# A two-layer MoE diffusion trunk: the last expert step of the second layer added by one-hot matmuls

## The chip, the cores and the metric

The kernel runs on one core of a Trainium2 chip. The metric is the device time of one execution in microseconds, as the median of several runs.

## What is computed

Two transformer layers over 128 context tokens and 512 latent tokens, 640 tokens of width 1024 in five tiles of 128 rows. All is float32. A layer is attention of three kinds and then a mixture of 16 experts, of which each token takes two. What matters here is the end of a layer and the final norm:

```python
x = x + gate2 * hier_moe(h, ...)          # each token: the sum of its two experts' rows
...
y_prompt = rms_norm(x_prompt, final_norm_g)
y_sample = rms_norm(x_sample, final_norm_g)
```

## The kernel before

PE is TensorE, DVE VectorE, ACT ScalarE, POOL GpSimd, SP the queue that issues most loads. The program is written out by hand for each engine, with semaphores between them; the order on an engine is the order of its code.

**Expert steps.** The 1280 pairs of token and expert are sorted by expert into slots, and 128 slots make a step. There are at least MIN_ET = 10 and at most N_ET = 18 steps; with this routing 15 are used in layer 0 and 14 (0 to 13) in layer 1. A step from 10 on stands under `if_used` (L493), a branch on the number of used steps; a skipped step still raises its semaphores by one (`else_inc`, L495 to L502). Step i does this:
- POOL gathers the 128 token rows from h_rows (L891).
- PE transposes them (`rows_T`), multiplies by the gate and up weights (`gate_up`, L2227, L2228 and L2233; a step of one expert has 8 matmuls of 128x512, one of two experts 16 on half the columns each), transposes the hidden rows (`hidden_T`), and multiplies by the down weights into PSUM banks 5 and 6 (`down`, L2268, L2269, L2275).
- DVE computes the hidden rows (`hidden`, L1743 to L1752), copies transposes (L1736, L1759), finishes the gate rows (L1763), and in `y_copy` (L1772) multiplies PSUM by slot weight and gate row into y_out[i % 2], two products of 128x512. Then y_evac_d counts i + 1.
- POOL's `y_store(i)` (L877) adds these rows to x_rows, the residual in HBM, by an indirect DMA with addition. It waits for y_evac_d and for the scatter before it, since two of them may hold the same token.

The loops are staggered: on DVE iteration i is `hiddenT(i-1)`, `rows_in(i+1)`, `hidden(i)`, `y_copy(i-1)`; on PE `gate_up(i)`, registers of step i + 1, `hidden_T(i-1)`, `rows_T(i+1)`, `down(i-1)`. `down(i)` waits for y_evac_d to reach i, since y_copy(i-1) reads the same banks. SP loads the experts' weights into four slots as the steps release them (L593, L597), and tells of their landing in order (L618).

**The end.** POOL waits for the landings of all used scatters and raises x_final (L907, L909). SP then loads the five tiles x_t from x_rows (L630), each with its own semaphore s_xin[t]. Per tile ACT sums squares (`final_sums`, L976), POOL forms the reciprocal root (L736, L741), DVE scales (`final_scale`, L1191), and SP stores the tile (L688).

The functions that the change touches follow, with the line numbers of the profile.

Of the kernel before, what the change touches and what calls it, by code (L numbers as in the profile page):

```python
# [21 lines left out]
P = 128  # L22
# [135 lines left out]
def trunk(nc, a, o):  # L158
# [9 lines left out]
    with ctx:  # L168
# [46 lines left out]
        rout_w = sb("rout_w", 2 * NT)  # L215
        tok_id = sb("tok_id", NT)
        lane = sb("lane", P)
        lane_w = sb("lane_w", 64)
        slots_i = sb("slots_i", 2 * NT, I32)
        w_slot = sb("w_slot", N_ET)  # L220
# [17 lines left out]
        b2b = arena[:, 2048:4096].rearrange("p (k n) -> p k n", k=2)  # L238
        gate2c = qT[:, 0:D]
        gain_f = arena[:, 0:1024]  # L240
        gain_b = q_tok[4]
        last_scaled = q_tok[4]
        a2b = arena[:, Q0 + 2 * D:Q0 + 4 * D].rearrange("p (k n) -> p k n", k=2)
# [51 lines left out]
        two = lane[:, 0:N_HALF:2]  # L295
        k_view = [k_tok[:, 640 * s:640 * (s + 1)] for s in range(2)]
        gate2l = modrow[:, 0:D]

        def hT_bank(t, r):
            return 1 if t == 0 and r == 1 else 7  # L300
# [392 lines left out]
        def _(pool):  # L693
            dma = pool.dma_start
            for v in (ident[:], wuk[:], sel64[:], k_tok[:]):
# [9 lines left out]
                      allow_small_or_imprecise_dtypes=True)  # L705
            pool.iota(k64, pattern=[[HALF, C_MAX]], base=0, channel_multiplier=0,
                      allow_small_or_imprecise_dtypes=True)
            pool.iota(tok_id[:], pattern=[[P, NT]], base=0, channel_multiplier=1,
                      allow_small_or_imprecise_dtypes=True)
            pool.iota(lane[:], pattern=[[1, P]], base=0, channel_multiplier=0,  # L710
# [71 lines left out]
            for l in range(DEPTH):  # L782
# [84 lines left out]

                def y_store(i):

                    with if_used(pool, i):  # L870
                        pool.wait_ge(y_evac_d[l], i + 1)
                        if i == 0:
                            pool.wait_ge(s_xout, (l + 1) * 16 * NT)
                        else:

                            pool.wait_ge(s_yout[l][(i - 1) % 2], 16 * ((i - 1) // 2 + 1))
                        pool.indirect_dma_start(  # L877
                            out=x_rows[l], out_offset=bass.IndirectOffsetOnAxis(ap=idx[:, i:i + 1], axis=0),
                            in_=y_out[i % 2], in_offset=None, compute_op=ALU.add
                        ).then_inc(s_yout[l][i % 2], 16)  # L880
# [22 lines left out]
                for i in range(N_ET - 3, N_ET):  # L903
                    y_store(i)

                for i in range(MIN_ET - 2, N_ET):
                    with if_used(pool, i):  # L907
                        pool.wait_ge(s_yout[l][i % 2], 16 * (i // 2 + 1))
                pool.sem_inc(x_final, 1)  # L909
                if l + 1 < DEPTH:  # L910
# [12 lines left out]
        def _(act):  # L923
# [48 lines left out]
                mod_copy(0, j)  # L972

            def final_sums(t):
                act.wait_ge(s_xin[t], 16 * DEPTH)
                act.activation(work[:, 1024 * (t % 2):1024 * (t % 2 + 1)], x_t[t], ACT.Square, scale=D ** -0.5,  # L976
                               accum_out=ssf[:, t:t + 1]).then_inc(f_ss, 1)
                act.drain()
# [196 lines left out]
        def _(dve):  # L1175
# [17 lines left out]
            for l in range(DEPTH):  # L1193
# [560 lines left out]
                def hiddenT(i):  # L1754
                    with if_used(dve, i):
                        dve.wait_ge(ht_done[l], i + 1)
                        if i >= 2:
                            dve.wait_ge(dn_done[l], i - 1)
                        cp(hidT[i % 2], ps[:, 4, 0:FF].rearrange("p (c n) -> p c n", c=2)).then_inc(ht_evac[l], 1)  # L1759

                        dve.wait_ge(lat_part[l], i + 1)
                        g = gate_rows[i % 2]
                        stt(g, gate2c, of_ctx[:, i:i + 1], g, ALU.mult, ALU.add)  # L1763

                def y_copy(i):
                    with if_used(dve, i):
# [2 lines left out]
                        y_buffer_free(dve, l, i)  # L1769
                        for k in range(2):  # L1770
                            half = slice(512 * k, 512 * (k + 1))
                            last = stt(y_out[i % 2][:, half], ps[:, 5 + k, :], w_slot[:, i:i + 1],  # L1772
                                       gate_rows[i % 2][:, half], ALU.mult, ALU.mult)
                        last.then_inc(y_evac_d[l], 1)
                    else_inc(dve, i, y_evac_d[l], 1, i)

# [2 lines left out]
                for i in range(N_ET + 1):  # L1779
# [8 lines left out]
                    if i >= 1:  # L1788
                        y_copy(i - 1)

            for t in range(NT):
                final_scale(t)


        @block.tensor
        def _(pe):
# [73 lines left out]
            for l in range(DEPTH):  # L1870
# [418 lines left out]
                for i in range(N_ET + 1):  # L2289
# [10 lines left out]
                    if i >= 1:  # L2300
                        down(i - 1)

_INS = ['x_prompt', 'x_sample', 'c', 'cache_mla_ckv', 'cache_mla_krope', 'cache_gqa_k', 'cache_gqa_v',
# [57 lines left out]
```

## Time and profile before

| | |
|---|---|
| median of 3 runs | 1450.79 us (1449.01 to 1451.2) |
| the profiled execution, its own time | 1446.95 us |
| its span | 1445.1 us |
| PE busy | 1269.4 us, 88% of the span |
| DVE busy | 728.3 us, 50% |
| ACT busy | 410.9 us, 28% |
| POOL busy | 226.9 us, 16% |

The profile is that of one execution; its times are counted from the start of its span. The shares are averages over stages with different limits: attention, weight loading and the expert steps each have their own. In the expert steps of layer 1, the last 190 us, the scatters follow each other at 11 to 19 us; the last two are at 1408 and 1416 us. A matmul of f32 operands stands in the profile as two records.

### The profile page before, as it was taken

What the parts mean: (1) busy time and instruction counts of PE and PEld (TensorE: products, weight loads), DVE (VectorE), ACT (ScalarE), POOL (GpSimd) and SP (SyncE); (2) the same over time, 40 slices, a digit from 0 to 9 for tenths busy, and PEclk for the clock granted to TensorE, in tenths of its full rate; (3) what the DMA queues carried; (4) which work ended last, traced back from release to release, by engine and by line L of the source; (5) the groups of instructions that cost most, each with busy time, mean ns of one, the idle gap of its engine ahead of it and who ended that gap; (6) DMA issues with size and microseconds to landing.
All of it is one profiled execution on the core that took longest, in us unless ns stands there. A gap on an engine that the chain in (4) does not pass through costs nothing. (4 is left out here: it accounts for less than half of the span.)

```text
span 1445.1 us, 22628 instructions
## 1 busy us (share of the span) xinstructions
PE 1269.4 (88%) x8172; PEld 758.8 (53%) x8172; DVE 728.3 (50%) x1741; ACT 410.9 (28%) x923; POOL 226.9 (16%) x325
## 2 busy tenths in 40 slices
PE   5899979999999959988959999899999992999981
PEld 4445546777767734433434554577776672444330
DVE  0344435776744545553514544466785437355442
ACT  2111135666610111111121110567664000111101
POOL 3310012010021112211111010210101111122212
PEclk8999999999999979999969999999999996999995
DMA  9800239000041797999950004670103233899955
GB/s 332 293 14 1 98 138 329 21 31 15 2 146 64 277 388 228 359 364 339 327 155 14 1 1 174 226 186 2 31 16 112 93 125 112 299 379 376 338 195 177
DMA packets 77996, 244.87 MB, mean 169 GB/s; under 512 B 9280, under 2 KB 19024, under 8 KB 65520
## 3 DMA queue, kind: packets, MB, share of 16 engines
q1 hardware_dynamic: 56080, 183.26, 34.1%
q0 software_dynamic: 17616, 58.44, 14.1%
q8 instruction: 101, 1.65, 0.5%
q10 hardware_dynamic: 4160, 1.20, 0.4%
q14 instruction: 39, 0.32, 0.1%
HBM read 213.54 MB, written 31.00 MB: 169 GB/s over the span
## 5 line engine op out<-in xcount | busy, mean ns | idle before, releaser
L1903 PE MATMUL ps<-ring,hT_region 128*128 128x512 f32 (+1 forms) x640 | 272.2, 582 | 3.4 <-ACT hT_region L988 3.4
L1903 PEld LDWEIGHTS ps<-ring,hT_region 128*128 128x128 f32 x640 | 121.6, 193 | 136.1 <-issue 135.5
L1352 DVE TENSOR_SCALAR_CACHE_REDUCE ring<-ps 128x768 f32<-128x768 f32 (+1 forms) x168 | 132.7, 820 | 119.1 <-PE ps L1976 92.6
L1041 ACT ACTIVATE ring<-ring,negm 128x768 f32<-128x768 f32 (+1 forms) x168 | 137.7, 820 | 30.9 <-DVE ring L1352 30.9
L2100 PE MATMUL ps<-ring,hT_region 128*128 128x384 f32 (+1 forms) x480 | 141.9, 452 | 0.0
L2233 PE MATMUL ps<-ring,hT_region 128*128 x272 | 125.4, 616 | 8.9 <-DVE hT_region L1736 4.6
L1976 PE MATMUL ps<-arena,qT 64*128 64x384 f32 (+1 forms) x640 | 124.8, 507 | 8.5 <-DVE ring L1352 2.9
L2100 PEld LDWEIGHTS ps<-ring,hT_region 128*128 128x128 f32 x480 | 89.6, 190 | 42.0 <-issue 0.3
L2029 PE MATMUL ps<-work,arena 128*64 128x128 f32 x1600 | 105.5, 278 | 6.0 <-ACT work L1057 4.3
L1057 ACT ACTIVATE work<-ps 128x512 f32<-128x512 f32 x128 | 75.8, 592 | 97.7 <-PE ps L1800 97.7
L2227 PE MATMUL ps<-ring,hT_region 128*64 x192 | 90.4, 626 | 13.4 <-SPq L618 13.4
L2029 PEld LDWEIGHTS ps<-work,arena 128*64 128x64 f32 x1600 | 86.1, 137 | 25.3 <-issue 15.0
L2233 PEld LDWEIGHTS ps<-ring,hT_region 128*128 128x128 f32 x272 | 52.8, 197 | 78.1 <-issue 78.1
L877 POOL DMA_INDIRECT x_rows<-arena,idx x29 | 47.0, 1620 | 297.1 <-DVE arena L1772 198.8
L1759 DVE COPY work<-ps 128x256 f32<-128x256 f32 x29 | 12.3, 424 | 161.2 <-PE ps L1800 161.2
L1137 ACT ACTIVATE work<-ps 128x256 f32<-128x256 f32 x29 | 11.1, 384 | 284.3 <-PE ps L2233 155.4
L2228 PE MATMUL ps<-ring,hT_region 128*64 128x512 f32 x192 | 90.4, 626 | 0.0
L1800 PE MATMUL ps<-ident,ring 128*128 128x128 f32 x600 | 82.3, 279 | 0.6 <-ACT work L1053 0.2
L1800 PEld LDWEIGHTS ps<-ident,ring 128*128 128x128 f32 x600 | 65.4, 141 | 28.6 <-issue 26.3
L1976 PEld LDWEIGHTS ps<-arena,qT 64*128 64x128 f32 (+1 forms) x640 | 56.1, 185 | 41.6 <-issue 18.5
L1227 DVE TENSOR_TENSOR work<-ps,rope 128x256 f32<-128x256 f32 (+2 forms) x40 | 14.0, 349 | 112.6 <-PE ps L1903 111.7
L2275 PE MATMUL ps<-arena,work 128*128 x136 | 64.5, 618 | 2.9 <-DVE work L1759 2.7
(322 smaller groups left out, 1776.8 us busy)
## 6 DMA issues: line engine op xcount, KB each, us to landing
ring<-in_w_mod SPq DMA_DIRECT2D x24, 2048.0 KB, 10.4
ring<-in_moe_w_gate SPq DMA_DIRECT2D x32, 1024.0 KB, 13.2
ring<-in_moe_w_up SPq DMA_DIRECT2D x32, 1024.0 KB, 17.0
arena<-in_moe_w_down SPq DMA_DIRECT2D x32, 1024.0 KB
ring<-in_w_in SPq DMA_DIRECT2D x6, 2048.0 KB, 19.9
arena<-mod_rows POOLq DMA_DIRECT2D x12, 512.0 KB, 6.2
x_rows<-x POOLq DMA_DIRECT2D x10, 512.0 KB, 3.0
h_rows<-work POOLq DMA_DIRECT2D x10, 512.0 KB, 2.9
```

The lines of the kernel that those rows point to most:

```text
L1041: act.activation(v, v, ACT.Exp, bias=negm[:, 2 * (k % 3) + m:2 * (k % 3) + m + 1], scale=-1.0, accum_out=sums[:, c:c + 1]).then_inc(exp_do ...
L1057: act.activation(to[:, 512 * b:512 * (b + 1)], ps[:, 4 + b, :], ACT.Copy).then_inc(pt_evac[b], 1)
L1352: ts(o_, i_, -pair_of(p)[4], None, ALU.mult, ALU.min, accum_out=col).then_inc(m_ready, 1)
L1800: return pe.transpose(out, in_, ident[:])
L1903: last = mm(ps[:, b, 0:n], hT[:, c, t * P:(t + 1) * P], w[:, c, :], start=(c == 0), stop=(c == KC - 1))
L1976: last = mm(ps[:, 2 * m + c, 0:384], q[r:r + n, :], kT[r:r + n, plane, 384 * c:384 * (c + 1)], start=True, stop=True)
L2029: last = mm(ps[64 * m:64 * (m + 1), 7, (u % 4) * P:(u % 4 + 1) * P], V[:, s_, vc:vc + 64], w[:, 768 * m + c * P:768 * m + (c + 1) * P], st ...
L2100: last = mm(ps[:, n % 4, 0:w_], oT[:, c, t * P:(t + 1) * P], w[:, c, :], start=(c == 0), stop=(c == KC - 1))
L2227: mm(g[0:HALF], h[:, c, 0:HALF], wa[:, c, :], start=(c == 0), stop=(c == KC - 1))
L2228: last = mm(g[HALF:P], h[:, c, HALF:P], wb[:, c, :], start=(c == 0), stop=(c == KC - 1))
L2233: last = mm(g, h[:, c, :], wa[:, c, :], start=(c == 0), stop=(c == KC - 1))
L2275: last = mm(ps[:, 5 + k, :], h[:, c, :], wa[:, c, k * 512:(k + 1) * 512], start=(c == 0), stop=(c == 1))
```

## The change

The last used step of layer 1 is no longer scattered. `y_store` and the wait behind the scatters test for step i + 1, so that the scatter of step i goes out only if another step follows; x_final comes behind the last but one. In the steps that may be the last (9 to 17) DVE writes the products to a buffer of its own, y_last, and copies that to y_out behind a drain; y_evac_d rises with the copy. In `hiddenT` of these steps it forms, from the step's row numbers and tile_base, a 128x128 matrix per tile that has a one where a slot's token is a row of that tile (last_hot). At the very end PE waits until y_evac_d is N_ET and multiplies each of the five matrices with y_last, in two halves, into PSUM; the fifth tile takes the first tile's banks and waits for DVE's first add. DVE adds PSUM to the loaded tile (`last_step`), and raises y_evac_d, on which `final_sums` now waits. The adds and scales on DVE are interleaved by hand.

```diff
--- before.py
+++ after.py
@@ -215,6 +215,7 @@
         rout_w = sb("rout_w", 2 * NT)
         tok_id = sb("tok_id", NT)
         lane = sb("lane", P)
+        tile_base = sb("tile_base", NT)
         lane_w = sb("lane_w", 64)
         slots_i = sb("slots_i", 2 * NT, I32)
         w_slot = sb("w_slot", N_ET)
@@ -238,6 +239,9 @@
         b2b = arena[:, 2048:4096].rearrange("p (k n) -> p k n", k=2)
         gate2c = qT[:, 0:D]
         gain_f = arena[:, 0:1024]
+        y_last = hT_region[:, 4096:5120]
+        last_hot = [k_tok[:, P * t:P * (t + 1)] for t in range(NT)]
+        last_at = k_tok[:, NT * P:NT * P + NT]
         gain_b = q_tok[4]
         last_scaled = q_tok[4]
         a2b = arena[:, Q0 + 2 * D:Q0 + 4 * D].rearrange("p (k n) -> p k n", k=2)
@@ -295,6 +299,9 @@
         two = lane[:, 0:N_HALF:2]
         k_view = [k_tok[:, 640 * s:640 * (s + 1)] for s in range(2)]
         gate2l = modrow[:, 0:D]
+
+        def last_rows(t):
+            return ps[:, 2 * (t % 4):2 * (t % 4) + 2, :].rearrange("p b n -> p (b n)")
 
         def hT_bank(t, r):
             return 1 if t == 0 and r == 1 else 7
@@ -705,6 +712,8 @@
                       allow_small_or_imprecise_dtypes=True)
             pool.iota(k64, pattern=[[HALF, C_MAX]], base=0, channel_multiplier=0,
                       allow_small_or_imprecise_dtypes=True)
+            pool.iota(tile_base[:], pattern=[[P, NT]], base=P, channel_multiplier=0,
+                      allow_small_or_imprecise_dtypes=True)
             pool.iota(tok_id[:], pattern=[[P, NT]], base=0, channel_multiplier=1,
                       allow_small_or_imprecise_dtypes=True)
             pool.iota(lane[:], pattern=[[1, P]], base=0, channel_multiplier=0,
@@ -867,7 +876,9 @@
 
                 def y_store(i):
 
-                    with if_used(pool, i):
+                    if l + 1 == DEPTH and i + 1 == N_ET:
+                        return
+                    with if_used(pool, i if l + 1 < DEPTH else i + 1):
                         pool.wait_ge(y_evac_d[l], i + 1)
                         if i == 0:
                             pool.wait_ge(s_xout, (l + 1) * 16 * NT)
@@ -903,8 +914,8 @@
                 for i in range(N_ET - 3, N_ET):
                     y_store(i)
 
-                for i in range(MIN_ET - 2, N_ET):
-                    with if_used(pool, i):
+                for i in range(MIN_ET - 2, N_ET if l + 1 < DEPTH else N_ET - 1):
+                    with if_used(pool, i if l + 1 < DEPTH else i + 1):
                         pool.wait_ge(s_yout[l][i % 2], 16 * (i // 2 + 1))
                 pool.sem_inc(x_final, 1)
                 if l + 1 < DEPTH:
@@ -972,7 +983,7 @@
                 mod_copy(0, j)
 
             def final_sums(t):
-                act.wait_ge(s_xin[t], 16 * DEPTH)
+                act.wait_ge(y_evac_d[DEPTH - 1], N_ET + t + 1)
                 act.activation(work[:, 1024 * (t % 2):1024 * (t % 2 + 1)], x_t[t], ACT.Square, scale=D ** -0.5,
                                accum_out=ssf[:, t:t + 1]).then_inc(f_ss, 1)
                 act.drain()
@@ -1761,6 +1772,14 @@
                         dve.wait_ge(lat_part[l], i + 1)
                         g = gate_rows[i % 2]
                         stt(g, gate2c, of_ctx[:, i:i + 1], g, ALU.mult, ALU.add)
+                        if may_be_last(i):
+                            tt(last_at, idx[:, i:i + 1].to_broadcast([P, NT]), tile_base[:], ALU.subtract)
+                            dve.drain()
+                            for t in range(NT):
+                                ts(last_hot[t], lane[:], last_at[:, t:t + 1], None, ALU.is_equal)
+
+                def may_be_last(i):
+                    return l + 1 == DEPTH and i + 1 >= MIN_ET
 
                 def y_copy(i):
                     with if_used(dve, i):
@@ -1769,8 +1788,11 @@
                         y_buffer_free(dve, l, i)
                         for k in range(2):
                             half = slice(512 * k, 512 * (k + 1))
-                            last = stt(y_out[i % 2][:, half], ps[:, 5 + k, :], w_slot[:, i:i + 1],
-                                       gate_rows[i % 2][:, half], ALU.mult, ALU.mult)
+                            last = stt((y_last if may_be_last(i) else y_out[i % 2])[:, half], ps[:, 5 + k, :],
+                                       w_slot[:, i:i + 1], gate_rows[i % 2][:, half], ALU.mult, ALU.mult)
+                        if may_be_last(i):
+                            dve.drain()
+                            last = cp(y_out[i % 2], y_last)
                         last.then_inc(y_evac_d[l], 1)
                     else_inc(dve, i, y_evac_d[l], 1, i)
 
@@ -1788,7 +1810,18 @@
                     if i >= 1:
                         y_copy(i - 1)
 
+            def last_step(t):
+                dve.wait_ge(s_xin[t], 16 * DEPTH)
+                dve.wait_ge(dn_done[DEPTH - 1], N_ET + t + 1)
+                tt(x_t[t], x_t[t], last_rows(t), ALU.add).then_inc(y_evac_d[DEPTH - 1], 1)
+
             for t in range(NT):
+                last_step(t)
+                if t >= 2:
+                    dve.drain()
+                    final_scale(t - 2)
+            dve.drain()
+            for t in (NT - 2, NT - 1):
                 final_scale(t)
 
 
@@ -2300,6 +2333,15 @@
                     if i >= 1:
                         down(i - 1)
 
+            pe.wait_ge(y_evac_d[DEPTH - 1], N_ET)
+            for t in range(NT):
+                if t == NT - 1:
+                    pe.wait_ge(y_evac_d[DEPTH - 1], N_ET + 1)
+                for k in range(2):
+                    last = mm(ps[:, 2 * (t % 4) + k, :], last_hot[t], y_last[:, 512 * k:512 * (k + 1)],
+                              start=True, stop=True)
+                last.then_inc(dn_done[DEPTH - 1], 1)
+
 
 
 _INS = ['x_prompt', 'x_sample', 'c', 'cache_mla_ckv', 'cache_mla_krope', 'cache_gqa_k', 'cache_gqa_v',
```

DVE, from the last step that may be used to the end of the program (before; names are out<-in by tile, idx and ps being the row numbers and PSUM):

```order
L493 COMPARE_AND_BRANCH
L1759 COPY work<-ps 128x256 [waits dn_done1,ht_done1]
L1763 SCALAR_TENSOR_TENSOR work<-qT,of_ctx,work 128x1024 [waits lat_part1]
L1755 UNCONDITIONAL_BRANCH
L493 COMPARE_AND_BRANCH
L1772 SCALAR_TENSOR_TENSOR arena<-ps,w_slot,work 128x512 [waits s_yout1_1,dn_done1]
L1772 SCALAR_TENSOR_TENSOR arena<-ps,w_slot,work 128x512
L1766 UNCONDITIONAL_BRANCH
L499 UNCONDITIONAL_BRANCH [waits y_evac_d1]
L1191 SCALAR_TENSOR_TENSOR x<-x,small,arena 128x1024 [waits f_rs,s_final] x5
```

The same step on DVE with the change:

```order
L1770 COPY work<-ps 128x256 [waits dn_done1,ht_done1]
L1774 SCALAR_TENSOR_TENSOR work<-qT,of_ctx,work 128x1024 [waits lat_part1]
L1776 TENSOR_TENSOR k_tok<-idx,tile_base 128x5
L1779 TENSOR_SCALAR k_tok<-lane,k_tok 128x128 x5
L1766 UNCONDITIONAL_BRANCH
L500 COMPARE_AND_BRANCH
L1791 SCALAR_TENSOR_TENSOR hT_region<-ps,w_slot,work 128x512 [waits s_yout1_1,dn_done1]
L1791 SCALAR_TENSOR_TENSOR hT_region<-ps,w_slot,work 128x512
L1795 COPY arena<-hT_region 128x1024
```

Six small instructions stand ahead of the branch that ends `hiddenT`, and a copy of 128x1024 stands behind the two products. The end of DVE's program with the change:

```order
L506 UNCONDITIONAL_BRANCH [waits y_evac_d1]
L1816 TENSOR_TENSOR x<-x,ps 128x1024 [waits dn_done1,s_xin0]
L1816 TENSOR_TENSOR x<-x,ps 128x1024 [waits dn_done1,s_xin1]
L1816 TENSOR_TENSOR x<-x,ps 128x1024 [waits dn_done1,s_xin2]
L1202 SCALAR_TENSOR_TENSOR x<-x,small,arena 128x1024 [waits f_rs,s_final]
L1816 TENSOR_TENSOR x<-x,ps 128x1024 [waits dn_done1,s_xin3]
L1202 SCALAR_TENSOR_TENSOR x<-x,small,arena 128x1024 [waits f_rs,s_final]
L1816 TENSOR_TENSOR x<-x,ps 128x1024 [waits dn_done1,s_xin4]
L1202 SCALAR_TENSOR_TENSOR x<-x,small,arena 128x1024 [waits f_rs,s_final] x3
```

Five adds have come in among the five scales. On PE the program ended with the skipped steps; with the change ten matmuls stand behind them:

```order
L506 UNCONDITIONAL_BRANCH [waits dn_done1]
L2341 MATMUL ps<-hT_region,k_tok 128x512 [waits y_evac_d1]
L2341 MATMUL ps<-hT_region,k_tok 128x512 x7
L2341 MATMUL ps<-hT_region,k_tok 128x512 [waits y_evac_d1]
L2341 MATMUL ps<-hT_region,k_tok 128x512
L168 UNCONDITIONAL_BRANCH
```

## Rows read from the trace of the kernel before

**Rows 1.** The chain that ended last, from 1408: start us, us, what.
```profile
1408.08 6.29 DMA x_rows<-arena,idx
...
1415.67 7.06 DMA x_rows<-arena,idx
...
1422.75 0.04 POOLq L907
...
1422.90 0.05 POOLq L493
...
1438.38 1.28 DVE x L1191
```

**Rows 2.** Timeline of DVE, steps 11 to 13: start us, us, engine line op.
```profile
1391.54 0.68 DVE L1736 COPY hT_region<-ps 128x512 f32<-128x512 f32 x1
...
1401.59 0.42 DVE L1759 COPY work<-ps 128x256 f32<-128x256 f32 x1 [4.77 <-PE ps L1800]
...
1406.39 1.41 DVE L1772 SCALAR_TENSOR_TENSOR arena<-ps,w_slot,qT 128x512 f32<-128x512 f32 x2 [0.16 <-PE ps L2269]
1407.72 0.41 DVE L1759 COPY work<-ps 128x256 f32<-128x256 f32 x1
1408.05 1.29 DVE L1763 SCALAR_TENSOR_TENSOR work<-qT,of_ctx,work 128x1024 f32<-128x1024 f32 x1
1413.98 1.41 DVE L1772 SCALAR_TENSOR_TENSOR arena<-ps,w_slot,work 128x512 f32<-128x512 f32 x2 [4.65 <-PE ps L2275]
```

**Rows 3.** Timeline of PE from gate_up(12) to down(13).
```profile
1379.48 1.11 PE L2227 MATMUL ps<-ring,hT_region 128*64 x1 [4.29 <-SPq L618]
...
1385.51 0.59 PE L2227 MATMUL ps<-ring,hT_region 128*64 x1
...
1390.76 3.69 PE L2275 MATMUL ps<-arena,work 128*128 x8
1394.29 7.03 PE L2233 MATMUL ps<-ring,hT_region 128*128 x16
...
1402.61 0.64 PE L2268 MATMUL ps<-arena,work 128*64 x1 [1.06 <-issue]
...
1408.55 5.39 PE L2275 MATMUL ps<-arena,work 128*128 x8 [1.41 <-DVE work L1759]
```

**Rows 4.** Busy time by stretch (PE, PEld, DVE, ACT, POOL), granted clock, DMA share, GB/s.
```profile
1379.00:1386.00 7.00, 6.52 (x18) 1.96 (x20) 0.00 (x0) 0.00 (x0) 0.33 (x1) 0.54 1.03 365
1409.00:1413.00 4.00, 4.00 (x7) 1.60 (x6) 0.34 (x1) 0.00 (x0) 0.64 (x1) 0.57 0.76 108
```

**Rows 5.** Timeline of the final stage, all engines.
```profile
1423.56 3.07 SPq L630 DMA_DIRECT2D x<-x_rows  x5
1427.77 1.06 ACT L976 ACTIVATE work<-x 128x1024 f32<-128x1024 f32 x1 [24.99 <-DMA x<-x_rows]
...
1429.34 0.57 POOL L741 TENSOR_TENSOR small<-small 128x1 f32<-128x1 f32 x1
...
1432.07 1.06 ACT L976 ACTIVATE work<-x 128x1024 f32<-128x1024 f32 x1 [0.51 <-DMA x<-x_rows]
...
1436.56 1.28 DVE L1191 SCALAR_TENSOR_TENSOR x<-x,small,arena 128x1024 f32<-128x1024 f32 x1 [0.53 <-POOL small L741]
1436.85 1.42 POOL L741 TENSOR_TENSOR small<-small 128x1 f32<-128x1 f32 x1
```

**Rows 6.** DVE groups by form: busy us, mean ns of one, idle before.
```profile
L1208 DVE TENSOR_SCALAR work<-x,small 128x1024 f32<-128x1024 f32 x10 | 7.5, 753 | 59.5 <-POOL small L741 59.1
...
L1407 DVE TENSOR_TENSOR hT_region<-hT_region,ps 128x512 f32<-128x512 f32 x10 | 6.8, 681 | 0.2
...
L1296 DVE TENSOR_SCALAR k_tok<-k_tok,small 128x128 f32<-128x128 f32 x10 | 2.9, 286 | 1.0
```

**Rows 7.** Timeline of DVE where layer 0's steps end and layer 1 begins.
```profile
723.94 1.41 DVE L1772 SCALAR_TENSOR_TENSOR arena<-ps,w_slot,qT 128x512 f32<-128x512 f32 x2 [2.92 <-PE ps L2275]
726.74 0.19 DVE L1198 TENSOR_TENSOR modcol<-ps,b1col 128x32 f32<-128x32 f32 x1 [1.39 <-DVEq L501]
```

## The prediction

> **What bounds the kernel now.** I read the end of the program first, because the change touches nothing before the second layer's last steps. The chain that ended last, taken over its last 40 us, shows which waits count [rows 1]. The reader is to see two scatter-adds one behind the other (6.29 us for step 12, 7.06 us for step 13, the last of the 14 steps used), then POOL's skipped branches, five of them at 0.15 us each (1422.75 to 1422.90 is one), then SP's loads of the residual tiles from 1423.56 on [rows 5], and at the very end the DVE's last final_scale, over at 1439.66. The change removes the last of these scatters from that chain. Second, DVE's own rows over steps 12 and 13 [rows 2]: DVE works from 1401.59 to 1409.34 and step 13's copy follows y_copy(12) without a gap, so what is added to it there moves what follows. Third, PE's rows at the same place and at an earlier wait [rows 3], with the granted clock [rows 4]: PE is idle for long before its last matmuls, and runs some at half clock. Fourth, the final stage [rows 5]: squares on ACT, roots on POOL, scales on DVE, one after the other per tile.
>
> **What is removed.** From the end of y_copy(13) (1413.98 + 1.41 = 1415.39 [rows 2]) to the end of the last scale (1439.66 [rows 1]) the kernel takes 24.3 us today. The scatter (1415.67 to 1422.73), the branches and the loads leave this path. With the wait moved to scatter 12, whose landing is at 1414.37 today, the loads start some 6 us earlier.
>
> **What is added ahead of the last step.** In each of steps 9 to 13 DVE computes last_at (128x5) and five one-hot matrices of 128x128, and copies y_last to y_out (128x1024).
> - One-hot matrices: no such compare is in the trace. The nearest row is a TENSOR_SCALAR on 128x128 with a column operand, 0.286 us alone [rows 6]; instructions that follow each other without a wait begin about 0.08 us before the one ahead is over (1407.72 behind 1406.39 + 1.41 [rows 2]), so some 0.23 each, 1.15 for five, and 0.25 for the small subtraction and the drain: 1.4 us. Bounds: 1.0 (half of 0.286 each) and 1.7 (0.286 each).
> - Copy: a one-input 128x1024 pass takes 0.75 us [rows 6], one with three operands 1.28 us [rows 1]. I take 0.85 with the drain, and keep 0.75 and 1.35. (y_copy itself has a drain ahead of it today, and the gap there is 0.16 us with a wait in it [rows 2]; 0.1 is my estimate from that.)
>
> Steps 9 to 11 hide this: PE waits 4.29 us for weights before gate_up(12) [rows 3], which takes up what the steps ahead of it are late; and before gate_up(13) DVE's copy of the gathered rows moves from an end at 1392.22 [rows 2] to 1393.6, while the first matmul starts at 1394.29 [rows 3]. That cover is 0.7 us; without it gate_up(13) would slip by the excess. Their scatters go out some 2.2 us later and are waited for by nothing that is late.
> In step 12 nothing hides it. The matrices (1.4) and the copy (0.85) both stand ahead of the copy of hidT(13), which moves from 1407.72 to 1410.0, and down(13) waits for it: PE from 1408.55 to 1410.8, **+2.25 us**. The matrices of step 13 lie under down(13). SP's queue has only the weights ahead, issued long before; POOL sends scatter 12 at 1410.3, it lands near 1416.6, the loads start 0.8 us later, near 1417.4, and the tiles land from 4.2 us after the first issue on (1423.56 to 1427.77 for tile 0, to 1432.07 for tile 2 [rows 5]), so at 1421.6 and 1425.9.
>
> **From down(13) to the last matmul.** down(13) takes 5.39 us today, part of it at half clock [rows 3, 4]; I keep that: end at 1416.2. (All at full clock 3.7, as its like at 1390.76 [rows 3]; all at half clock 6.9.) y_copy(13) 1.45, its copy 0.85: 1418.5. Now PE waits for y_evac to reach 18, and DVE gets there only through the skipped steps 14 to 17. Layer 0 shows the price: after y_copy(14) of 15 used steps, 5 branches and 3 increments pass before the next instruction, 1.39 us (725.35 to 726.74 [rows 7]). Here it is 9 branches and 4 increments: 1.39 + 4 x 0.155 (POOL's branch, rows 1) + 0.1 = **2.1 us**; by branches alone 2.5. PE starts at 1420.7.
> The ten matmuls are f32, 128x512: the trace has two records of one each (down(13): four matmuls, x8), every 0.43 us at full clock and 0.855 at half. So 20 records: 8.6 us at full clock. PE has then been idle for 4.5 us. Before gate_up(12) it was idle for 4.29 us, and then seven records (pairs on half the columns each, of the same length) ran at half clock, from 1379.48 to 1385.51, before the pace doubled [rows 3, 4]. I take the same: tiles 0 to 4 are ready at 1424.3, 1427.3, 1429.0, 1430.7 and 1432.5.
>
> **The final stage.** DVE now has ten passes of 128x1024 instead of five: the adds (128x512 from PSUM is 0.68 us [rows 6], so some 1.22) and the scales (1.28). They queue: from tile 2 on DVE has add 2, scale 0, add 3, scale 1, add 4, scale 2, scale 3 without a gap: 1429.0 + 7 x 1.26 + 0.4 for the drains = 1438.2. Today the root for the last tile comes 0.44 us behind the end of scale 3 (POOL's pow takes 1.42 us beside a scale, 0.57 alone [rows 5]), and scale 4 starts 0.54 us behind it: 1438.8 to **1440.1**, against 1439.66. The stores follow as today, 5.4 us to the end of the span.
> The Trainium skill, SBUF — State Buffer, section "Who interferes with whom", has a lock behind this: a Vector instruction with two SBUF inputs and a GpSimd instruction that reads SBUF exclude each other, the later one blocks. The 1.42 against 0.57 us agrees; without the lock the end would be at 1439.6, not at 1440.1. The same page says that an fp32 SBUF to SBUF copy on DVE keeps GpSimd from writing the descriptors of its DMAs, which speaks against the added copy; POOL sends each scatter behind that copy, so it meets only the matrices, and scatter 12 has some 3 us to spare.
>
> **Sum.** Up to the end of y_copy(13)'s two products +2.25 (1417.65 for 1415.39); from there to the end of the last scale 22.4 in place of 24.3, -1.85; together **+0.4 us**. The profiled execution would take 1446.95 + 0.4 = 1447.4; the median of the runs shown is 3.8 us above that execution, so I forecast 1450.79 + 0.4 = 1451.2 us. What a measurement of this kernel can tell from no change is about 0.2%, 2.9 us.
>
> **The rivals.**
> - *The clock is kinder* (chance 0.15 for faster by over 2.9 us): down(13) at full clock throughout (-1.7) and four half-clock records at the end instead of seven (-1.3) give +0.4 - 3.0 = -2.6; with cheap matrices (-0.4) -3.0, 1447.8 us, and with an unblocked root (-0.5) 1447.3. For it: the half-clock stretches in the trace differ in length, under 4 us in down(13) [rows 4] and 6.0 in gate_up(12) [rows 3]. Against: PE is idle for some 2 us before down(13) and 4.5 before the last ten, and all three must come together.
> - *The clock holds the last matmuls back* (0.27 for slower by over 2.9 us): place, the ten matmuls; price, 0.43 us for each further record at half clock up to the twelfth, since tile 2 then comes later and seven passes of DVE stand behind it. Twelve slow records come to +2.6 in all; all twenty to +4.0 (tile 4 at 1438.0, then add 4 and three scales). With down(13) at half clock too (+1.5) it crosses 2.9 us from ten slow records on, or with the seven if the copy, which is on this path twice, has its upper price. 1453.7 to 1456.
> - *The skipped steps on PE decide* (inside the first forecast's range): PE also passes steps 15 to 17, with register loads. If they take longer than DVE's 4.4 us, up to +2. Against: between gate_up(13) (over at 1401.32) and down(12) at 1402.61 stand a step's register loads, its branches and two transposes, 1.3 us in all [rows 3]; three such steps are 3.9 us.
> - *The change does not do what it says*: the loads may end last after all. They have 3 us of slack [rows 5]; nothing speaks for it, and it would cost 1 us at most, inside the first forecast.
>
> **The numbers.** Within 0.2%: 0.58, the forecast with every other cost inside its bounds; faster 0.15, slower 0.27, for there are more added costs without a row of their own than savings. The range 1447.5 to 1455.5 takes in the kind clock and most of the unkind one.
>
> **What would show it.** Step 12: down(13) starting 2.2 us later against gate_up(13). No scatter on the chain's end; the chain going through DVE's skipped branches (2.1 us) to PE's last matmuls. 20 records of 0.43 or 0.855 us. DVE gapless from add 2 to scale 3. The tiles landed before the matmuls. I would be wrong if PE started its ten matmuls before 1418 or if DVE waited for tile 3 or 4.

## The result: 0.52% slower

The changed kernel took 1455.33 us (median of 12 runs, 1449.58 to 1463.0), the kernel before 1449.44 us beside it. The ratio is 1.0052, with a 95% interval of 1.0037 to 1.0067, so some 7.5 us (5.4 to 9.7) where +0.4 us was forecast. (The ratio is not the quotient of the two medians, which lie 5.9 us apart; the means lie 7.5 us apart. Where one kernel is set against another below, it goes by the ratios.) The range was counted from 1450.79 us, so it reached from -3.3 to +4.7 us: 7.5 us is above it, though 1455.33 us as such is not. It is in the case "slower by over 0.2%", to which a chance of 0.27 was given for another reason than the one found. The profiled execution took 1452.8 us, with a span of 1450.9 us.

**The profile after.** First DVE's timeline over steps 12 and 13 up to the last adds, which answers to [rows 2].

```profile
1398.85 0.42 DVE L1770 COPY work<-ps 128x256 f32<-128x256 f32 x1 [2.77 <-PE ps L1833]
...
1400.39 0.16 DVE L1776 TENSOR_TENSOR k_tok<-idx,tile_base 128x5 f32<-128x5 int32 x1
1400.63 1.07 DVE L1779 TENSOR_SCALAR k_tok<-lane,k_tok 128x128 f32<-128x128 f32 x5
...
1406.36 0.69 DVE L1795 COPY arena<-hT_region 128x1024 f32<-128x1024 f32 x1
1406.97 0.42 DVE L1770 COPY work<-ps 128x256 f32<-128x256 f32 x1
...
1413.24 1.41 DVE L1791 SCALAR_TENSOR_TENSOR hT_region<-ps,w_slot,work 128x512 f32<-128x512 f32 x2 [3.42 <-PE ps L2308]
1414.72 0.69 DVE L1795 COPY arena<-hT_region 128x1024 f32<-128x1024 f32 x1
1431.55 1.22 DVE L1816 TENSOR_TENSOR x<-x,ps 128x1024 f32<-128x1024 f32 x1 [16.13 <-PE ps L2341]
```

Step 12 now has the matrices (1.22 us with their subtraction) and the copy ahead of step 13's copy at 1406.97. Up to y_copy(13) all is as forecast. Then DVE idles for 16.1 us, until PE's last matmuls bring the first tile. PE's own timeline (it answers to [rows 3]) and SP's loads of the residual tiles ([rows 5]):

```profile
1407.81 5.39 PE L2308 MATMUL ps<-arena,work 128*128 x8 [2.53 <-DVE work L1770]
1427.68 11.25 PE L2341 MATMUL ps<-hT_region,k_tok 128*128 128x512 f32 x20 [14.47 <-PEq L508]
```
```profile
1414.46 2.50 SPq L637 DMA_DIRECT2D x<-x_rows  x5
```

The ten matmuls (20 records) begin 13.0 us after y_copy(13)'s products are over (1413.24 + 1.41 = 1414.65); 3.05 us was forecast (1417.65 to 1420.7). The idle time ends on "PEq L508": PE's own instruction queue, at the increment of a semaphore in a skipped step. The loads of the residual tiles are issued at 1414.46 and land in 8.1 us (median), long before 1427.68: they are not the cause.

Which of the two queues is late? The increments of the skipped steps (line 508) and their branches (line 500), from 1409 to 1430; the columns are the count, the shortest, median and longest in ns, and the first and last start:

```profile
L508 PEldq EVENT_SEMAPHORE  x6: 51/51/51, 1413.8 to 1427.6; - x6
L508 DVEq EVENT_SEMAPHORE  x4: 21/21/21, 1416.0 to 1418.0; - x4
```
```profile
L500 DVEq COMPARE_BRANCH  x15: 50/56/63, 1409.1 to 1417.8; - x15
L500 PEldq COMPARE_BRANCH  x12: 208/208/3688, 1412.8 to 1425.2; - x12
```

DVE, which the forecast took for the late one, is through at 1418.0, 2.6 us after its copy's end (1415.41); 2.1 was forecast, with 2.5 as the upper price. PE is through at 1427.65. Most of its branches take 208 ns, but one takes 3688 ns. The same line in three short stretches (1413.9 to 1416.5, 1420.2 to 1424.1, 1425.1 to 1427.6) shows three long ones:

```profile
L500 PEldq COMPARE_BRANCH  x1: 2607/2607/2607, 1414.0 to 1414.0; - x1
...
L500 PEldq COMPARE_BRANCH  x1: 3688/3688/3688, 1420.3 to 1420.3; - x1
...
L500 PEldq COMPARE_BRANCH  x2: 208/1248/2288, 1425.0 to 1425.2; - x2
```

Together 2.61 + 3.69 + 2.29 = 8.6 us. Between the first two stand the four register loads of one skipped step, from 1416.8 to 1419.3:

```profile
L2239 PEldq TENSOR_LOAD <-experts_i x4: 295/297/298, 1416.8 to 1418.7; - x4
```

With the instructions that go with each they take 2.5 us. The remaining 3.4 us of the 14.5 are short branches, increments and the wait for down(13) itself to be counted. The same was to be seen in the kernel before, where nothing waited for it at the program's end; these rows of its trace (1409 to 1430, there lines 493 and 501) were not read ahead of the forecast:

```profile
L493 PEldq COMPARE_BRANCH  x13: 208/213/2527, 1409.3 to 1423.9; - x13
```
```profile
L501 PEldq EVENT_SEMAPHORE  x7: 51/51/51, 1409.6 to 1426.3; - x7
```

PE's last increment is at 1426.3, 12.4 us after down(13) was over (1408.55 + 5.39, [rows 3]). At the border of the two layers PE even waited for it:

```profile
732.48 1.09 PE L1800 MATMUL ps<-ident,k_tok 128*128 128x128 f32 x4 [8.57 <-PEq L501]
```

From the start of step 12's copy to the end of the last scale the profiled executions take 38.07 us before (1401.59 to 1439.66) and 47.22 after (1398.85 to 1446.07), +9.15. Up to the end of y_copy(13)'s products +2.0 of it, behind that +7.15 (31.42 for 24.27). All ahead of that copy was 2.7 us earlier in this execution, by what one execution differs from the next: the 12 runs of the changed kernel lie up to 13.4 us apart.

### The profile page after: what moved, and what is told of

It reads as the page before. It is cut to its first block and busy times, and to the rows that moved or that the text cites. A ratio compares the mean times of both kernels' runs of the same rounds, so it can differ in the third digit from the quotient of the medians.

```text
span 1450.9 us, 22725 instructions
## 1 busy us (share of the span) xinstructions
PE 1278.9 (88%) x8192; PEld 762.2 (53%) x8192; DVE 743.1 (51%) x1781; ACT 410.6 (28%) x923; POOL 222.9 (15%) x325
## 5 line engine op out<-in xcount | busy, mean ns | idle before, releaser
L2260 PE MATMUL ps<-ring,hT_region 128*64 x192 | 87.3, 609 | 11.2 <-SPq L625 11.2
L1148 ACT ACTIVATE work<-ps 128x256 f32<-128x256 f32 x29 | 11.1, 383 | 278.9 <-PE ps L2266 155.3
L2261 PE MATMUL ps<-ring,hT_region 128*64 128x512 f32 x192 | 87.3, 609 | 0.0
```

What stands on the lines that cost most here:

```text
L2260: mm(g[0:HALF], h[:, c, 0:HALF], wa[:, c, :], start=(c == 0), stop=(c == KC - 1))
L2261: last = mm(g[HALF:P], h[:, c, HALF:P], wb[:, c, :], start=(c == 0), stop=(c == KC - 1))
```

## The experiments

I call "stretch" what was just used: from the start of DVE's copy in step 12 to the end of the last scale, in the profiled execution. The theory: PE's skipped steps decide, and in them the far branches, behind each of which the code has to be fetched. Rivals: DVE's skipped steps, the register loads of the skipped steps, or the number of branches.

**PE without the skipped steps.** In layer 1 PE's loop ends behind step 13, and four increments are made up behind a wait:

```diff
-                for i in range(N_ET + 1):
-                    if i < N_ET:
+                ends = 14 if l + 1 == DEPTH else N_ET
+                for i in range(ends + 1):
+                    if i < ends:
...
+                if l + 1 == DEPTH:
+                    pe.wait_ge(dn_done[l], ends)
+                    pe.sem_inc(dn_done[l], N_ET - ends)
```

> The changed kernel, with PE's loop over the second layer's steps ending at step 14 (steps 14 to 17 are not used by this routing, so nothing is left out here; dn_done is raised by the missing 4 in one go). Theory A, PE's own way through the skipped steps held the ten matmuls back: the first of them starts within 0.3 us of DVE's y_evac_d reaching 18, so some 9.5 us earlier than in the changed kernel, and the time falls by 7 to 10 us, to 1446 to 1448. Theory B, DVE's skipped steps (2.6 us behind the copy) or the clock held them back: no change beyond 1 us, 1455.

Measured: 1447.7 us, ratio 0.9988 (0.9971 to 1.0006), so some 9 us less than the changed kernel by the two ratios. PE's last rows:

```profile
1413.04 6.43 PE L2308 MATMUL ps<-arena,work 128*128 x8 [2.43 <-DVE work L1770]
1424.37 11.04 PE L2345 MATMUL ps<-hT_region,k_tok 128*128 128x512 f32 x20 [4.90 <-DVEq L508]
```

Now the wait ends on DVE's queue, and the matmuls start 3.45 us behind y_copy(13)'s products (1420.92), where 3.05 was forecast. The stretch is 38.37 us, against 38.07 before: this is the kernel that the forecast had in mind, with its +0.3 for +0.4 us (the ratio says -1.7 us, with an interval that takes in both). That the two agree so closely is luck in part: up to the end of the products it took 0.7 us more than forecast, because down(13) took 6.43 us in this execution and not 5.39, and behind them 0.8 us less (21.63 for 22.4).

**DVE without the skipped steps**, the same edit on DVE's loop with y_evac_d (`dve.wait_ge(y_evac_d[l], ends)`, `dve.sem_inc(y_evac_d[l], N_ET - ends)`).

> The changed kernel, with DVE's loop ending at step 14 in the second layer instead of PE's, y_evac_d raised by 4 in one go. Theory A: the matmuls start where they did, 14 us behind the end of down(13), the time stays at 1455 within 1 us. Theory B: they start 2.6 us or more earlier and the time falls by as much.

Measured: 1455.99 us, ratio 1.005 (1.0034 to 1.0067), no better than the changed kernel.

```profile
1427.86 10.53 PE L2345 MATMUL ps<-hT_region,k_tok 128*128 128x512 f32 x20 [12.92 <-PEq L508]
```

PE waits for its own queue, as before, and the time doesn't fall: DVE's skipped steps alone are worth nothing here. The wait is 1.55 us shorter than in the changed kernel, though PE's program is the same: its three long branches took 2.31, 2.83 and 1.87 us, 7.0 us in all for 8.6. So far can the same branches differ from one execution to the next.

**Short jumps.** The matmuls behind the branches of steps 14 to 17, which are never run, are cut to one or two, and the inner branches on a step's form, which aren't run either, go with them; the branches that are run, register loads and increments stay:

```diff
+                        if short(i):
+                            mm(g, h[:, 0, :], wa[:, 0, :], start=True, stop=True).then_inc(gu_done[l], 1)
+                        else:
...
+                def short(i):
+                    return l + 1 == DEPTH and i >= 14
```

> The changed kernel, with the bodies of gate_up and down of the steps 14 to 17 of the second layer cut to one and two matmuls; these bodies are jumped over with this routing, and all branches, register loads and semaphores stay. Theory A1, what costs is how far PE's branch jumps (the code behind it has to be fetched): the branches of 2.3 to 3.7 us shrink to the 0.2 us of the others, the matmuls start 8 to 10 us earlier, time 1446 to 1449. Theory A2, the number of branches or the register loads cost: less than 1 us of gain.

Measured: 1448.25 us, ratio 0.9993 (0.998 to 1.0005). The branches and PE's last rows:

```profile
L500 PEldq COMPARE_BRANCH  x16: 65/204/367, 1410.0 to 1425.7; - x16
```
```profile
1426.08 11.86 PE L2351 MATMUL ps<-hT_region,k_tok 128*128 128x512 f32 x20 [6.41 <-PEq L508]
```

No branch is longer than 0.37 us, and the wait is 6.4 us instead of 14.5. So it isn't the number of branches: it is how far they jump. (The instruction queue moves two packets between 1400 and 1445 us, where it moves six in the changed kernel.) PE still ends last, 1.6 us behind DVE (1424.5): branches, loads and increments of the skipped steps at close range cost it 6.4 us.

**No register loads** for steps 14 to 17 (they keep the values of step 13, which nothing reads):

```diff
                 def step_registers(i):
+                    if l + 1 == DEPTH and i >= 14:
+                        form[i], last_e[i], at_ring[i], at_arena[i] = (
+                            v[13] for v in (form, last_e, at_ring, at_arena))
+                        return
```

> The changed kernel without the four register loads of each of the steps 14 to 17 on PE in the second layer. A1: these loads stand beside the long branches and give at most 1.5 us, 1454 to 1455. A3, the loads are what costs: the matmuls start 5 us or more earlier, time below 1451.

Measured: 1455.72 us, ratio 1.0032 (1.0015 to 1.005); the interval overlaps that of the changed kernel.

```profile
L500 PEldq COMPARE_BRANCH  x13: 208/214/4348, 1410.6 to 1424.7; - x13
```
```profile
1427.46 11.29 PE L2345 MATMUL ps<-hT_region,k_tok 128*128 128x512 f32 x20 [11.23 <-PEq L508]
```

The wait is 11.2 us instead of 14.5, 3.2 us less in this one execution. Not all of it need be the loads': down(13) took 6.46 us here for 5.39 and hid more of the passage, and counted from its start the matmuls begin 2.2 us sooner. The loads' own rows above, 2.5 us behind down(13), fit with both. The far branches are there still: 1.54, 4.35 and 2.59 us behind down(13).

**What the far branches do to the kernel before.** There nobody waits for PE at the end, so cutting PE's loop should change nothing. The edit is that of the first experiment, without what was added behind the loop.

> The kernel before, with PE's loop ending at step 14 in the second layer. Theory A: PE's way through the skipped steps ends at 1426.3 in the kernel before and nothing waits for it, so the time does not change: ratio 1.000 within 0.15%. If the ratio fell to 0.998 or less, the skipped steps would cost by another way than the wait that the change added.

Measured: 1445.52 us, ratio 0.9977 (0.996 to 0.9995). This was not expected. The DMA queues between 1400 and 1445 us show where a path may be: fetched code travels by DMA too. Queues and loads of the kernel before, then of this one (packets, MB, share of the 16 DMA engines; last row KB each and median us to landing):

```profile
q8 instruction: 6, 0.10, 1.0%
...
x<-x_rows SPq DMA_DIRECT2D x5, 512.0 KB, 6.8
```
```profile
q8 instruction: 1, 0.02, 0.2%
...
x<-x_rows SPq DMA_DIRECT2D x5, 512.0 KB, 5.3
```

Six packets of some 16 KB against one, and a slower scatter 13 (7.06 us [rows 1] against 6.26) and slower loads. From 1423 to 1428 the DMA engines are 0.56 busy at 164 GB/s before and 0.87 at 318 GB/s here:

```profile
1423.00:1428.00 5.00, 0.00 (x0) 0.00 (x0) 0.00 (x0) 0.23 (x1) 0.00 (x0) 0.50 0.56 164
```
```profile
1423.00:1428.00 5.00, 0.00 (x0) 0.00 (x0) 0.00 (x0) 1.66 (x3) 0.45 (x2) 0.50 0.87 318
```

Part of that is only that the loads are issued 1 us later before; 1 us further on, from 1424 to 1429, it is 0.74 at 240 GB/s there. From the end of y_copy(13) to the last scale it takes 22.1 us against 24.3. Three more sets of runs put this to the test. The same kernel again, with more runs:

> The same kernel as e5_before_pe_no_skipped, once more with more runs, because its 0.23% gain was not expected. Leaves out PE's skipped steps 14 to 17 of layer 2 of the kernel before. Theory C (the fetches of code that TensorE's far branches cause travel beside scatter 13 and the loads of x and slow them): the instruction queue moves 1 packet in place of 6 between 1400 and 1445 us, scatter 13 takes about 6.3 us in place of 7.06, the loads land in about 5.3 us in place of 6.8 (median), and the ratio is 0.997 to 0.999 with its interval below 1. Rival (chance of one set of runs): ratio 0.9995 to 1.0005, and the durations of scatter and loads spread without regard to the fetches.

Measured: 1446.33 us, ratio 0.9985 (0.9966 to 1.0003); one packet, scatter 13 6.25 us, loads 5.3 us, 22.1 us from y_copy(13) on. The kernel before with the short jumps of the third experiment:

> The kernel before with the matmuls behind the skipped branches of steps 14 to 17 of layer 2 cut to one or two, so that each branch jumps a short way; branches and register loads stay, and nothing in this kernel waits for TensorE there. Theory C: the ratio is that of e9_before_pe_again within 0.1%, the instruction queue moves fewer packets in the tail than in the kernel before (6), and scatter 13 and the loads are as quick as in e9_before_pe_again. Rival (it is the branches or register loads themselves, or chance): ratio 1.000 within 0.05% while e9_before_pe_again stays at 0.998.

Measured: 1447.07 us (11 of 12 runs; the twelfth, with 1480.49 us, is left out), ratio 0.9989 (0.997 to 1.0008); two packets, scatter 13 6.33 us, loads 6.2 us, 22.4 us. And the kernel before with PE's steps nested, so that one branch passes over all that is left (the edit is shown with the next experiment):

> The kernel before, with TensorE's steps nested behind one branch in both layers, as in e6_nested, and nothing else. It tells how much of what e11_best_again gains over the kernel before is due to the far branches alone and how much to the last step added by TensorE. Theory: the gain of e9_before_pe_again (0.1 to 0.3%) or a little more, since layer 1's end has the same far branches before the next layer's first matmul, which waits 8.57 us there: ratio 0.996 to 0.999. If e11_best_again is lower still, by 0.1% or more, the difference is the TensorE add's own gain. Rival: 1.000, the nest costs as much in one far jump as the skipped steps did.

Measured: 1446.38 us, ratio 0.9988 (0.9964 to 1.0011); four packets, scatter 13 6.14 us, loads 5.2 us, 22.4 us. All four come out lower, by 1.6 to 3.3 us, and all four profiles have the quick scatter 13 and a shorter tail; but only one interval excludes 1, there is one profile of the kernel before, and only one of its six packets lies under scatter 13. Quick loads don't follow the count of packets closely either (6.2 us with two, 5.2 with four).

Scatter 12 tells more. In the nested kernel three packets of code lie under it, and it takes 7.33 us; it took 6.29 in the kernel before, with one:

```profile
1407.57 7.33 DMA x_rows<-arena,idx
```

So it is in all the kernels of this record: with none to two packets under it scatter 12 takes 6.3 to 6.7 us (nine profiles), with three, in the five nested ones (this one and the four below), 7.3 to 7.7 us. Fetched code beside a scatter goes with some 1 us more for it once there are three packets; no run parts the fetches from the rest of what nesting changes, and how much of the few us above is theirs stays open.

**A mend that any routing allows.** PE's loop is nested, in both layers, from step 10 on: a step that isn't used jumps once, over all later ones, and the increments are made up at the jump's end:

```diff
-                for i in range(N_ET + 1):
+                def part(i):
...
+                def finish(n):
+                    if n < N_ET:
+                        for signal in (gu_done[l], dn_done[l]):
+                            pe.wait_ge(signal, n)
+                            pe.sem_inc(signal, N_ET - n)
+
+                def parts_from(i):
+                    with pe.If(tiles_used[pe] > i - 1):
+                        part(i)
+                        if i < N_ET:
+                            parts_from(i + 1)
+                        else:
+                            finish(N_ET)
+                    with pe.Else():
+                        finish(i - 1)
```

> The changed kernel, with PE's iterations behind step 10 nested: one branch on the number of used steps skips all that is left, and one increment brings gu_done and dn_done to 18, in both layers, for any routing. Theory A1: one far branch (2 to 4 us) in place of several, over before DVE's count reaches 18, so the matmuls start within 0.3 us of it: -7 to -9 us in the second layer, and up to -3 more at the border of the layers, where PE waits 8.6 us behind the same branches: 1444 to 1448, ratio 0.996 to 0.999. If it is the jumped distance alone that costs, one jump over all of the code could cost as much as before: then no gain.

Measured: 1446.21 us, ratio 0.9981 (0.9963 to 0.9998), some 10 us less than the changed kernel. PE's matmuls wait 4.90 us for DVE's queue, exactly as with the skipped steps cut away. At the border of the layers PE's wait falls from 8.57 to 3.8 us, of which 1.7 us is only that down(14) ahead of it took 5.39 us for 3.70.

Next, the ten matmuls stand inside that branch, at the end of the last used step, and wait for y_copy of that step alone (`pe.wait_ge(y_evac_d[l], n)` in `finish`), not for DVE's count of 18:

> As the nested kernel, and the ten matmuls stand behind the branch of their step and wait for y_evac_d of that step, no longer for 18: DVE's skipped steps (2.6 us) leave the path too. The matmuls start 0.1 us behind the copy or one far branch (2 to 4 us) behind down(13), whichever is later: -2 us against the nested kernel, ratio 0.9945 to 0.9975. If the loads of the tiles (landing 5 to 8 us behind their issue) end last, the gain is 1 us or less.

Measured: 1445.07 us, ratio 0.9957 (0.9935 to 0.998).

```profile
1422.50 10.55 PE L2349 MATMUL ps<-hT_region,k_tok 128*128 128x512 f32 x20 [2.27 <-DVE arena L1795]
```

The matmuls begin right behind the copy (over at 1422.44); from y_copy(13)'s products to the last scale it takes 18.5 us instead of 31.4. Six runs stand behind the ratio. Last, what was added to step 12 is taken away again: the matmuls read y_out of the step itself, so the copy is gone, and the matrices are built only in a step that is the last one:

```diff
-                        if may_be_last(i):
-                            tt(last_at, idx[:, i:i + 1].to_broadcast([P, NT]), tile_base[:], ALU.subtract)
...
+                        if may_be_last(i) and i + 1 < N_ET:
+                            with dve.If(tiles_used[dve] < i + 2):
+                                hot(i)
+                        elif may_be_last(i):
+                            hot(i)
...
-                        if may_be_last(i):
-                            dve.drain()
-                            last = cp(y_out[i % 2], y_last)
```

> As the one before, without y_last and its copy (the matmuls read y_out of their step) and with the one-hot matrices only where a step is the last. The copy (0.69 us, twice on the path) and the matrices of step 12 (1.3 us) leave the path, a branch (0.1) comes in, all else equal: -2 to -2.7 us against the one before, ratio 0.993 to 0.996; if by then the loads of the tiles or DVE's ten passes decide alone, -1 or less.

Measured: 1441.8 us (7 runs), ratio 0.9966 (0.9944 to 0.9988): outside what was expected (0.993 to 0.996), and no lower than the one before it (0.9957), though its median is 3.3 us lower. In the profiles the stretch is 3.9 us shorter, 0.9 of which is down(13) (5.39 us for 6.33). So the traces show the gain of this last step, and the times don't. And once more, with more runs:

> The same kernel as e8_best, once more with more runs, for the interval: ratio 0.995 to 0.998 against the kernel before, interval below 1 (the profiled execution of e8_best was 7.8 us under that of the kernel before, the medians 0.35 to 0.5% under). If it was a lucky set: 0.998 to 1.000.

Measured: 1442.57 us, ratio 0.9962 (0.9941 to 0.9982): 5.5 us faster than the kernel before and some 13 us faster than the change as it was made. Against the kernel before nested (0.9988) it is 0.26% lower, in the same set of runs, but the intervals overlap. The rows at the end, from the first of the two profiles:

```profile
1408.15 5.39 PE L2310 MATMUL ps<-arena,work 128*128 x8 [1.25 <-DVE work L1770]
1415.04 8.85 PE L2352 MATMUL ps<-arena,k_tok 128*128 128x512 f32 x20 [1.50 <-DVEq L508]
```
```profile
1419.57 3.72 DVE L1819 TENSOR_TENSOR x<-x,ps 128x1024 f32<-128x1024 f32 x3 [4.58 <-DMA x<-x_rows]
```

PE's wait is 1.5 us. The row names DVE's queue, but what the matmuls wait for is the count that the products raise, over at 1414.99. DVE now waits for the loads of the residual tiles, which lie behind scatter 12 (7.44 us in its chain, issued at 1407.76): what bounds the end is once more a scatter and the loads, and this scatter is one of those with three packets of code under them. In the second profile it took 7.66 us and DVE waited for a tile twice, so that the stretch was 32.40 us and not 31.26.

| profiled execution | to the end of y_copy(13)'s products | behind it | stretch | PE's wait, ended by |
|---|---|---|---|---|
| before | 13.80 | 24.27 | 38.07 | none |
| the change | 15.80 | 31.42 | 47.22 | 14.47, PE's queue |
| PE without skipped steps | 16.74 | 21.63 | 38.37 | 4.90, DVE's queue |
| DVE without them | 15.80 | 29.14 | 44.94 | 12.92, PE's queue |
| short jumps | 15.77 | 23.95 | 39.72 | 6.41, PE's queue |
| no register loads | 16.78 | 28.21 | 44.99 | 11.23, PE's queue |
| nested | 15.70 | 21.76 | 37.46 | 4.90, DVE's queue |
| and the last step inside | 16.64 | 18.51 | 35.15 | 2.27, DVE's copy |
| and no extra copy | 13.72 | 17.54 | 31.26 | 1.50, DVE's products |

The first column holds chance, too: down(13) took 5.39 us in most of these executions, and 6.33 to 6.46 in three of them (PE without skipped steps, no register loads, the last step inside).

## Why the prediction was wrong

The step that failed is the second one under "From down(13) to the last matmul": "Now PE waits for y_evac to reach 18, and DVE gets there only through the skipped steps". PE passes the same skipped steps, and needs 14.5 us for it behind down(13), not the 3.9 us that the third rival gave it ("up to +2"). That price was 1.3 us a step, taken from the gap between gate_up(13) and down(12), where the step is used and no branch passes over its matmuls. A branch that jumps over them is another thing: 8.6 of the 14.5 us are three such branches. A row with the right one was in the trace (PE's branches at line 493, up to 2.5 us; PE's wait of 8.57 us at the layers' border), and only DVE's row of that border was read [rows 7]. PE starts its matmuls 10.0 us later behind y_copy(13) than forecast; the final stage behind that start gives 1.0 back (18.4 us for 19.4), and 9.0 is the whole miss of that part (+7.15 for -1.85).

Point by point:
- **Step 12**: +2.0 for +2.25 us. Matrices 1.22 with the subtraction (1.4 forecast), copy 0.69 (0.85). The row at 1400.63 puts each matrix at 0.21 us, which is also what the forecast's own numbers give (0.286 - 0.08; it says 0.23). Right.
- **The loads issued earlier**: right in kind, 14.46 for 17.4 with the execution 2.7 us ahead. They land in 8.1 us (median) where it was 6.8 before, and are waited for by nothing.
- **DVE's skipped steps**: 2.6 us for 2.1. The price by branches alone (2.5) was the better one. (1418.5 + 2.1 makes 1420.6, not 1420.7; nothing hangs on it.) It would have been the bound, had PE been quick: the first experiment shows it.
- **The last ten matmuls**: 20 records, as forecast, 11.25 us; at 0.43 us each they would take 8.6, so some six were at half clock, where seven were forecast. The granted clock is 0.50 from 1428 to 1432 and 0.96 from 1432 to 1440. PE had idled for 14.5 us; behind 4.9 us it was 11.0, and behind 1.5 us, in the best kernel, 8.85, all at full clock (1.00 from 1415 to 1424). Between these the time doesn't follow the idle time: 10.5 us behind 12.9 and behind 2.3 us, 11.9 behind 6.4. The rival "the clock holds the last matmuls back" did not come about.
- **DVE's queue of adds and scales**: right, with gaps of 0.17 us at most from the third add at 1435.60 to the end, 10.5 us for 11.1.
- **The root beside a scale**: 1.42 us was forecast for the last, it took 0.57:

```profile
1443.25 0.26 POOL L745 TENSOR_SCALAR small<-small 128x1 f32<-128x1 f32 x1 [1.67 <-ACT work L987]
1443.59 0.57 POOL L750 TENSOR_TENSOR small<-small 128x1 f32<-128x1 f32 x1
```
```profile
1443.59 2.48 DVE L1202 SCALAR_TENSOR_TENSOR x<-x,small,arena 128x1024 f32<-128x1024 f32 x2 [0.16 <-issue]
```

It starts at the same moment as scale 3. The long roots of [rows 5] start while a scale is under way; the other four here start while an add of PSUM is under way, and take 0.57 us too. The Trainium skill, SBUF — State Buffer, section "Who interferes with whom", has the later of the two instructions blocked; with the starts equal, neither is seen to lose here. The forecast's 0.5 us for it was not paid.

With PE's passage priced from its own rows, 12.4 us behind down(13), the sum would have been: down(13) over at 1416.2, the matmuls from 1428.6 instead of 1420.7, +7.9 us, so +8.3 in place of +0.4. Measured: +7.5.

The rows tell that the far branches are long and that packets of code go with them, not how. The Trainium skill has a mechanism, on its page Runtime: NRT & Kernel Launch, section "Instruction fetch mechanics": a taken branch whose target lies outside the pages of code at hand forces a fetch by DMA before execution goes on. The traces agree: 1.5 to 4.3 us for a far branch, mostly 0.2 for a near one, and packets of 16 KB on the instruction queue that fall from six to two or one with the far branches gone. The prices come from these rows.

## What to carry to other kernels

Before an engine is given work behind steps that may be skipped, look at that engine's own branches and increments in the trace, with their longest times and not the median: PE, with nothing behind it, hid 12 us there, and they come to light when something is queued behind them. On TensorE put such work inside the branch that ends the used steps, or jump once over all that is left rather than once per step; and let it wait for the step it needs, not for a count that another engine reaches through its own skipped steps. Of the change's idea, trading a scatter for ten matmuls, what is left once neither wait is in the way is 0.26% against the kernel before with the same nest, with intervals that overlap; the 0.38% against the kernel before itself has the nest's own part in it.

## What the runs showed of the hardware

- A branch on PE mostly costs 0.208 us (up to 0.44) at close range. Where it passes over a step's matmuls it takes 1.5 to 4.3 us, three times behind down(13) in the changed kernel (8.6 us in all, 7.0 in another execution of the same program of PE). DVE's take 0.056 us, POOL's 0.045, with at most 0.063 in these stretches.
- A register load on PE takes 0.30 us, 0.63 us with what goes with it; the four of one skipped step take 2.5 us. Without any the wait was 3.2 us shorter (14.47 against 11.23, one execution each).
- The profile counts fetched code, in packets of 16 KB, among the DMA engines' work. With three such packets under it scatter 12 took 7.3 to 7.7 us (five profiles), with none to two 6.3 to 6.7 (nine). With PE's far branches out of the kernel before, its time fell by 0.1 to 0.2%, at the edge of what was measured.
